# Hybrid decoder trunk: expert items of 96 token slots instead of 128, and up to three turns for an expert

## The reference, cut to what matters

```
logits = (xn @ w_router)                      # (256, 8)
top_v, top_i = lax.top_k(logits, 2)
top_w = softmax(top_v)
gates = sum(one_hot(top_i, 8) * top_w[..., None])
for e in range(8):
    out = out + gates[..., e:e+1] * swiglu(xn, w_gu[e], w_down[e])
```

## Time and the profile before

| | us |
|---|---|
| median of 3 runs | 1548.2 (1546.65 to 1552.72) |
| span of the profiled execution | 1545.4 |
| the eight items, in that span | 580.0 to 1528.55 |
| PE busy in the span | 1486.9 |
| DVE, ACT, POOL busy | 1200.6, 1010.6, 152.7 |

### The profile page before, as it was taken

The page is one execution under the profiler, slowest core; times in us unless marked ns, Lnnn a source line. Parts: engine busy times, 40 slices in busy tenths (PEclk is TensorE's granted clock), DMA queues, the critical chain, the costliest instruction groups (busy, mean ns, idle before and its releaser), DMA issues.

```text
span 1545.4 us, 22764 instructions
## 1 busy us (share of the span) xinstructions
PE 1486.9 (96%) x8592; PEld 1293.8 (84%) x8592; DVE 1200.6 (78%) x1039; ACT 1010.6 (65%) x973; POOL 152.7 (10%) x165
## 2 busy tenths in 40 slices
PE   8999899999997889999999999999999999999995
PEld 7998899998995588888888888888888888888884
DVE  6854555556457748898889888888888888988887
ACT  5743444344446847777777778777777777777775
POOL 0600000000203618000000000000000000001001
PEclk9999999999998999999999999999999999999998
DMA  9760255556987028999999999999999999999992
GB/s 302 227 211 2 96 179 164 193 189 175 178 246 288 2 84 335 411 403 396 374 378 390 367 375 379 392 368 390 389 373 386 381 372 388 389 370 378 410 379 110
DMA packets 176777, 456.66 MB, mean 295 GB/s; under 512 B 11187, under 2 KB 72844, under 8 KB 176722
## 3 DMA queue, kind: packets, MB, share of 16 engines
q1 hardware_dynamic: 171234, 436.29, 76.3%
q0 software_dynamic: 5312, 19.47, 4.8%
q10 hardware_dynamic: 176, 0.14, 0.0%
HBM read 437.52 MB, written 16.78 MB: 294 GB/s over the span
## 4 chain that ended last, share of the span: by engine, by line
PE 93%; DVE 2%; ACT 2%; issue 1%; DMA 1%; POOL 0%; ACTq 0%; POOLq 0%; DVEq 0%
PE ps L1677 91%; PE ps L2076 2%; DVE arena L1500 1%; DVE arena L1497 0%; PE ps L2142 0%; ACT arena L1141 0%; DMA arena<-item_rows,arena 0%; DMA arena<-in_norm_mix_g 0%; ACT x_hi L940 0%; PE ps L1688 0%; PE ps L1925 0%; ACT x_hi L970 0%; DVE arena L1501 0%; ACT between L1162 0%; POOL arena L812 0%
## 5 line engine op out<-in xcount | busy, mean ns | idle before, releaser
L567 DVE TENSOR_TENSOR w_lo<-ring,w_hi 128x2048 fp32r<-128x2048 f32 x339 | 774.2, 2291 | 107.1 <-ACT w_hi L563 105.8
L563 ACT ACTIVATE w_hi<-ring 128x2048 fp32r<-128x2048 f32 x339 | 650.9, 1920 | 237.3 <-PE ps L1677 236.2
L1677 PE MATMUL ps<-w_hi,x_hi 128*128 128x512 f32 (+1 forms) x1056 | 337.0, 383 | 2.7 <-DVE x_lo L1576 2.7
L1677 PE MATMUL ps<-w_hi,x_lo 128*128 128x512 f32 (+1 forms) x1056 | 333.5, 380 | 0.0
L1677 PE MATMUL ps<-w_lo,x_hi 128*128 128x512 f32 (+1 forms) x1056 | 284.0, 380 | 0.0
L1677 PEld LDWEIGHTS ps<-w_hi,x_lo 128*128 128x128 f32 x1056 | 198.7, 188 | 37.6
L1677 PEld LDWEIGHTS ps<-w_lo,x_hi 128*128 128x128 f32 x1056 | 198.6, 188 | 37.5
L1677 PEld LDWEIGHTS ps<-w_hi,x_hi 128*128 128x128 f32 x1056 | 196.3, 188 | 39.5 <-issue 4.5
L516 DVE TENSOR_TENSOR w_lo<-ring,w_hi 128x2048 fp32r<-128x2048 f32 x67 | 153.3, 2291 | 77.2 <-ACT w_hi L510 77.1
L510 ACT ACTIVATE w_hi<-ring 128x2048 fp32r<-128x2048 f32 x67 | 127.6, 1910 | 101.9 <-PE ps L1677 96.7
L1677 PE MATMUL ps<-w_hi,hid 128*128 128x512 f32 x768 | 191.4, 391 | 0.0
(11 more groups left out here) (262 smaller groups left out, 1188.7 us busy)
## 6 DMA issues: line engine op xcount, KB each, us to landing
ring<-in_moe_w_gu SPq DMA_DIRECT2D x224, 1024.0 KB, 6.5
ring<-in_moe_w_down SPq DMA_DIRECT2D x112, 1024.0 KB, 6.2
ring<-in_ffn_w_gu SPq DMA_DIRECT2D x22, 1024.0 KB, 5.1
ring<-in_a_w_in SPq DMA_DIRECT2D x16, 1024.0 KB, 10.8
ring<-in_ffn_w_down SPq DMA_DIRECT2D x11, 1024.0 KB, 5.0
ring<-in_w_kv SPq DMA_DIRECT2D x6, 1024.0 KB, 5.1
item_rows<-hT SPq DMA_DIRECT2D x12, 512.0 KB, 9.2
ring<-in_a_w_out SPq DMA_DIRECT2D x4, 1024.0 KB, 5.5
```

Of the source, the lines that this page charges most:

```text
L563: eng.activation(w_hi[:, m % PAIRS, :], ring[:, m % RING, :], ACT.Copy).then_inc(hi_ready[m % PAIRS], 1)
L567: eng.tensor_tensor(w_lo[:, m % PAIRS, :], ring[:, m % RING, :], w_hi[:, m % PAIRS, :].bitcast(F32), ALU.subtract).then_inc(lo_ready[m % P ...
L1677: return pe.matmul(o, w, x, start=start, stop=stop, **kw)
```

## The change

Items hold 96 slots. An expert may have three turns of 96; the table of possible items is wider (3 x 8 candidates), the row arithmetic on POOL gains a third term, and `item_rows` has 13 items of 96 rows. All areas that hold slots on partitions become 96 partitions high; those that hold slots along the free dimension become 96 wide. What moves through TensorE in the item's products is still 512 columns of weights.

```
-TILE = 128
+TILE = 96
 TURNS = -(-T // TILE)
 ITEMS = 16
-assert E + 2 * T // TILE < ITEMS and TURNS == 2
+assert E + 2 * T // TILE < ITEMS and TURNS == 3
...
-        x_rows, item_x = area(0, TT, D), area(8000, D)
+        x_rows, item_x = area(0, TT, D), area(8000, D, parts=TILE)
...
-        HM = area(4096, WIDE)
-        SU = area(5120, WIDE)
+        HM = area(4096, WIDE, parts=TILE)
+        SU = area(5120, WIDE, parts=TILE)
         hid_wide = [hid[:, part, :, :].rearrange("p b n -> p (b n)") for part in range(2)]
-        hid_last = [v[:, KC * TILE:KC * TILE + 512] for v in (x_hi, x_lo)]
-        yt = area(6144, D)
+        hid_last = [v[:, KC * TILE:KC * TILE + 4 * TILE] for v in (x_hi, x_lo)]
+        yt = area(6144, D, parts=TILE)
...
-                sp.dma_start(item_rows.ap()[n], hT[:, 0:KC // 2, :].rearrange("p c t -> p (c t)")).then_inc(rows_set, 16)
+                sp.dma_start(item_rows.ap()[n], hT[0:TILE, 0:KC // 2, :].rearrange("p c t -> p (c t)")).then_inc(rows_set, 16)
...
-                while n > 1:
+                while n >= TURNS:
                     link(pool.tensor_tensor(prod[:, :, 0:n], prod[:, :, 0:n], prod[:, :, n:2 * n], ALU.add))
                     n //= 2
+                for n in range(2, TURNS):
+                    link(pool.tensor_tensor(prod[:, :, 0:1], prod[:, :, 0:1], prod[:, :, n:n + 1], ALU.add))
                 link(pool.tensor_tensor(dst.unsqueeze(2), prod[:, :, 0:1], prod[:, :, 1:2], ALU.add))
...
-            link(pool.tensor_scalar(first_row, incl[:, 0:E], float(TILE), -float(TILE), ALU.mult, ALU.add))
-            link(pool.tensor_scalar(second_row, incl[:, E:2 * E], float(TILE), -2.0 * TILE, ALU.mult, ALU.add))
-            link(pool.tensor_tensor(second_row, second_row, first_row, ALU.subtract))
-            link(pool.tensor_scalar(at_row, pos, float(TILE), None, ALU.is_ge))
-            link(pool.tensor_tensor(at_row, at_row, second_row.unsqueeze(1).to_broadcast([P, TT, E]), ALU.mult))
+            turn_rows = (first_row, second_row, third_row)
+            for n, v in enumerate(turn_rows):
+                link(pool.tensor_scalar(v, incl[:, E * n:E * n + E], float(TILE), -float((n + 1) * TILE), ALU.mult, ALU.add))
+            for n in (2, 1):
+                link(pool.tensor_tensor(turn_rows[n], turn_rows[n], turn_rows[n - 1], ALU.subtract))
+            for n in (1, 2):
+                v = at_row if n == 1 else row_turn
+                link(pool.tensor_scalar(v, pos, float(n * TILE), None, ALU.is_ge))
+                link(pool.tensor_tensor(v, v, turn_rows[n].unsqueeze(1).to_broadcast([P, TT, E]), ALU.mult))
+            link(pool.tensor_tensor(at_row, at_row, row_turn, ALU.add))
...
-                        dst = hid_wide[0][:, 512 * n:512 * n + 512] if j < LAST else hid_last[0]
-                        act.activation(dst, ps[:, b, :], ACT.Copy).then_inc(hid_hi, 1)
+                        dst = hid_wide[0][:, 4 * TILE * n:4 * TILE * n + 4 * TILE] if j < LAST else hid_last[0]
+                        act.activation(dst, ps[:, b, 0:4 * TILE], ACT.Copy).then_inc(hid_hi, 1)
...
-                        dve.tensor_tensor(HM[:, 512 * n:512 * n + 512], SU[:, 512 * n:512 * n + 512], ps[:, b, :], ALU.mult).then_inc(bank_free[b], 1)
+                        dve.tensor_tensor(HM[:, 512 * n:512 * n + 512], SU[:, 512 * n:512 * n + 512], ps[0:TILE, b, :], ALU.mult).then_inc(bank_free[b], 1)
...
-                            last = pe.transpose(ps[:, b, P * c:P * c + P], HM[:, at:at + P], ident)
+                            last = pe.transpose(ps[:, b, TILE * c:TILE * c + TILE], HM[:, at:at + P], ident[0:TILE, 0:TILE])
...
-                                mm(ps[:, b, :], hidden[part][:, P * c:P * c + P], wh[:, at:at + 512],
+                                mm(ps[0:TILE, b, :], hidden[part][:, TILE * c:TILE * c + TILE], wh[:, at:at + 512],
...
-                                mm(ps[:, b, :], x[:, ks * q + k, :], wh[:, width * k + 512 * n:width * k + 512 * n + 512],
+                                mm(ps[0:TILE, b, :], x[:, ks * q + k, :], wh[:, width * k + 512 * n:width * k + 512 * n + 512],
...
-                            last = pe.transpose(ps[:, b, TILE * c:TILE * c + TILE], item_x[:, at:at + P], ident)
+                            last = pe.transpose(ps[:, b, TILE * c:TILE * c + TILE], item_x[:, at:at + P], ident[0:TILE, 0:TILE])
```

More of the change, by code:

```diff
@@ L408, in trunk @@
         row_at = area(7492, TT, 2).bitcast(U32)
+        third_row, row_turn = area(7512, E), area(7520, TT, E)
         row_gap, row_later = area(7504, TT, 1), area(7506, TT, 1)
@@ L1232, in _ @@
                                 kept(act, i)
-                            act.activation(yt[:, 512 * n:512 * n + 512], ps[:, b, :], ACT.Copy).then_inc(bank_free[b], 1)
+                            act.activation(yt[:, 512 * n:512 * n + 512], ps[0:TILE, b, :], ACT.Copy).then_inc(bank_free[b], 1)
                     item_refill_hi(act, m, i)
@@ L1244, in _ @@
                             act.wait_ge(bank_free[bu], ku + 1)
-                            act.activation(SU[:, 512 * n:512 * n + 512], ps[:, b, :], ACT.Silu).then_inc(bank_free[b], 1)
+                            act.activation(SU[:, 512 * n:512 * n + 512], ps[0:TILE, b, :], ACT.Silu).then_inc(bank_free[b], 1)
                     if ITEM[m] in TURN_AT:
@@ L1632, in hidden_lo @@
                         dve.wait_ge(hid_hi, FFN // 256 + i * HIDDEN + sum(BANKS_OF[:j]) + n + 1)
-                        dst, hi = (v[:, 512 * n:512 * n + 512] for v in (hid_wide[1], hid_wide[0])) if j < LAST else (hid_last[1], hid_last[0])
-                        dve.tensor_tensor(dst, ps[:, b, :], hi.bitcast(F32), ALU.subtract).then_inc(bank_free[b], 1)
+                        dst, hi = (v[:, 4 * TILE * n:4 * TILE * n + 4 * TILE] for v in (hid_wide[1], hid_wide[0])) if j < LAST else (hid_last[1], hid_last[0])
+                        dve.tensor_tensor(dst, ps[:, b, 0:4 * TILE], hi.bitcast(F32), ALU.subtract).then_inc(bank_free[b], 1)
                 def hidden_product(j):
@@ L2101, in down_chunk @@
                             final = j == LAST and c == 4 * BANKS_OF[j] - 1
-                            last = mm(ps[:, b, :], hidden[0][:, P * c:P * c + P], wl[:, at:at + 512], False, final)
+                            last = mm(ps[0:TILE, b, :], hidden[0][:, TILE * c:TILE * c + TILE], wl[:, at:at + 512], False, final)
                             if final:
@@ L2120, in input_chunk @@
                             final = q == GU_CHUNKS[j] - 1 and k == ks - 1
-                            last = mm(ps[:, b, :], xg_hi[:, ks * q + k, :], wl[:, width * k + 512 * n:width * k + 512 * n + 512], False, final)
+                            last = mm(ps[0:TILE, b, :], xg_hi[:, ks * q + k, :], wl[:, width * k + 512 * n:width * k + 512 * n + 512], False, final)
                             if final:
```

## The result

The changed kernel takes 1562.79 us (median of 4 runs, 1561.68 to 1563.29) against 1547.43 us for the kernel before in the same comparison (4 runs, 1544.38 to 1552.72): a ratio of 1.0089, 95% interval 1.007 to 1.0108. It is slower, by 0.9% where 0.5% of gain was forecast. A second comparison with more runs gave 1.008 (1.0063 to 1.0097).

A forecast was written before the change was run, and what follows sets the result against it. TensorE's own stream was taken to bound the items; gains of 7.7 us (transposes), 0.3 (ahead of the items) and 0.4 (after them) made 8.4, so 1548.2 - 8.4 = 1539.8 us, 0.54% faster, range 1525 to 1550.

The forecast's parts named there:

- What bounds the kernel, and that eight items run: Whole kernel: only TensorE's own stream moves the time within items; items stay 8, a ninth would cost 118.5 us.
- The products: 4032 products in the items: the 13.4 ns over the moving columns' time is fixed, so narrower stationary blocks change 0 us.
- The two bounds from rows: Limits on the items' products: 13.4 us gained if the excess follows stationary columns, 107.5 us lost if loads are slow.
- the rival on slow loads: Items' products: weight loads of 96 columns take 64 cycles more, 26.7 ns a product, +107.5 us, 1647 us; chance 0.08.
- something small that becomes late: Rival: something like POOL's longer chain or the DMA ring runs late, 0.5 to 1% slower, 1556 to 1564 us; chance 0.07.
- The rival by which the excess goes with the stationary columns: Items' products: their excess shrinks with the stationary columns, 13.4 us more gained, 1526.4 us; chance 0.09.
- The transposes: 288 transposes in the items: the moving side sets their pace, 109 ns falls to 82.3, gaining 7.7 us.
- Ahead of the items: Before the first item: ACT and DVE handle a quarter fewer columns, gaining 0.3 us; the gather gains 0.
- POOL's longer chain, the extra store, ACT, DVE and DMA at nothing: POOL's 6 more operations, 13 stores for 12, and ACT, DVE and DMA in the items hold nothing up: 0 us.
- After the items: Tail: the last store of `yt` shrinks from 512 to 384 KB, so POOL waits less, gaining 0.4 us.
- The signs by which to tell: Profile marks of error: 144 products above 33 or below 32.3 us, 8 transposes at 0.87, longer ACT DMA wait, 126 down chunks.

The follow-up runs named there:

- The fourth experiment: The kernel before, 128 slots, its products reading blocks of 128 columns that start 96 columns apart, so its output is not the model's: 1576.79 us (one run).

## Why the prediction was wrong

**What bounds the kernel, and that eight items run: right.** TensorE's own stream set the time after the change too, and 112 down chunks were loaded again.

**The products: the step that failed.** "So I take it as fixed: 0 for the 4032 products." The excess of a product over its 512 moving columns went from 13.5 ns to 18.1. By the best pace of both kernels that is 4.6 x 4032 = 18.5 us of stream; by the rows of the chain, which hold the slower products behind transposes too, it is 2.04 x 8 = 16.3 us. The step had looked at one thing, whether the excess scales with the clock, and took "does not scale" for "does not depend on the stationary side". It depends on the width, on where the blocks start and on the number of moving columns. The two bounds from rows, a quarter less or a slow load, did not bracket it either: between a gain of 13.4 us and a loss of 107.5 lay a loss of 16 with no rival of its own. The mechanism of the rival on slow loads, a load that takes longer, is refuted: the load's record fell from 188 to 162 ns. The measured 1562.79 us lies in the range of another rival, something small that becomes late (1556 to 1564), but that is luck: inside the items neither POOL's chain nor the DMA ring was late, and the one small thing that was, the tail, makes 1.1 us. The rival by which the excess goes with the stationary columns was right for products of 256 moving columns (13.2, 9.2 and 6.7 ns at 128, 96 and 64) and wrong for the 512 of this kernel.

**The transposes: right.** 82.3 ns were forecast and about 82 measured, 7.7 us gained, and with 86 slots a transpose took the 74 ns that the same sum gives. Its moving columns and its rows shrink together in every version, so that it is the columns and not the rows is argued and not shown.

**Ahead of the items: right in the operations** (0.25 us less for ACT and DVE against 0.3), but nothing of it reached the time in the first profile. The two profiles of the changed kernel start their items 4.1 us later and 0.9 earlier than that of the kernel before, and the change's own 0.3 is lost in that.

**POOL's longer chain, the extra store, ACT, DVE and DMA at nothing: right.** None of them appears in the chain inside the items.

**After the items: wrong in sign.** 0.4 us less was forecast; the tail was 1.1 to 1.2 us longer in both profiled executions of the changed kernel and 0.8 to 1.4 in those of the versions with full-width products (POOL waits 2.76 to 2.79 us for the store instead of 2.42, its next operation takes 1.0 us instead of 0.48). The fourth experiment, which has the places 96 apart but the store of 128 rows, waits 2.43 us and takes 0.47, so it goes with the smaller store and not with the products. Why a smaller store should be waited for longer is open.

**The signs by which to tell** served: "more than 33 us for 144 products" was the mark of the error, and the profile crossed it.

What stays open is why the place and the width count. That the two reads of TensorE get in each other's way fits the shifts at width 128 (with a period of 256 bytes), but the runs do not show which part of the memory or of TensorE would make them wait, nor why narrower blocks cost time at 512 moving columns and save it at 256, nor why 112 columns have two paces in the whole kernel.

## What to carry to other kernels

Fewer stationary columns are no sure gain for a TensorE product: in fp32r they made it 1 to 3% dearer at 512 moving columns, 2% cheaper at 448 and 3 to 5% cheaper at 256. Where products move 512 columns, let them run over all 128 stationary ones and narrow only what moves, such as the identity of a transpose; here that was worth 0.24%. Keep the blocks of the stationary operand and the starts of the moving one 256 bytes apart or a multiple of that. Before a shape changes in a stream of thousands of equal instructions, measure that one shape by itself: one kernel of 20 stretches gave the whole table, and a few ns in each product outweighed every other term.

## What the runs showed of the hardware

- The spacing of fp32r products isn't the moving columns plus a constant: with the full width the excess is 13.2 to 13.6 ns at 512, 384, 320 and 256 columns, and 19.8 ns at 448.
- Narrow stationary operands are faster at 256 moving columns (113.4 ns at 64 and 112 against 119.9 at 128) and slower at 512 (229.0 to 233.4 against 226.7).
- At width 128 and 512 moving columns a shift of 128 bytes on one of the two operands costs 5.6 to 5.8 ns a product; on both together it costs 0.4.
- The span of one and the same kernel goes with its mean granted clock: the kernel before spans 1542.3 us at 0.984 and 1555.1 at 0.976.
